# A two-layer hybrid decoder step: compression products spread over the first eight steps of prompt attention

## The chip, the cores and the metric

The kernel runs on one core of one Trainium2 chip, in float32. The metric is the device time of one launch in microseconds (us), taken as the median of several runs. A profiled execution is one more run, taken by the hardware profiler; its span is the time from its first to its last recorded instruction.

A core has five engines that matter here: TensorE (PE; its weight loads are PEld), VectorE (DVE), ScalarE (ACT), GpSimd (POOL) and SyncE (SP). Each works through its own queue of instructions in order; where an instruction needs another engine's result it waits on a semaphore, and everything behind it on that engine waits too. Data comes from device memory by DMA; here SyncE issues the loads of weights and GpSimd the gathers of the caches.

## The reference, cut to what matters

Two request groups share the weights: one prompt of 512 tokens, and 8 sampled sequences of 4 new tokens each, with 2048 past tokens in paged caches. Each of the two layers has a recurrent group (RG-LRU) beside an attention group with three branches, an output projection and a gated ConvFFN. What the change touches is the attention group, sampled and prompt:

```
def _compress(rows, pe, w1, b1, w2):            # 32 rows -> one compressed row, every 16 rows
    ua = einsum('bnshd,sdf->bnhf', ch + pe[:16], w1[:16])
    ub = einsum('bnshd,sdf->bnhf', ch + pe[16:], w1[16:])
    hid = gelu(ua[:, :-1] + ub[:, 1:] + b1)
    return einsum('bnhf,fd->bnhd', hid, w2)

def _nsa_core(...):
    p_cmp = masked_softmax(q_c . kc);  o_cmp = p_cmp . vc          # compressed rows
    idx = top_k(block sums of p_cmp, 16)
    o_slc = masked_softmax(q_r . ks[idx]) . vs[idx]                # selected blocks of 64 rows
    o_win = masked_softmax(q_r . kw) . vw                          # the last 512 rows
    return gates . (o_cmp, o_slc, o_win)
```

The sampled sequences compress their whole compressed-branch cache in every layer (8 sequences of 2048 rows), read all pages of the selected-branch cache, and mask the blocks that were not selected. The prompt compresses its own 512 rows.

## The kernel before, in words

**One layer.** Projections, RG-LRU and the key and value projections come first; then compression; then a planned stretch of attention; then the output projection and the ConvFFN. The dense products (line 377) take most of TensorE's time and are not touched.

**Compression.** The list `compressed_units` (line 283) has nine units: seven sampled caches ("cmp" 0 to 6), the prompt's own rows ("cmpp"), and the eighth sampled cache. For one sampled cache GpSimd issues four gathers into a 16 KB slot of `ar` (`cache`, line 1064; three slots in turn), VectorE transposes the rows in two instructions (`turn_chunks`, lines 1627 and 1633), and TensorE forms two products, v = 0 for keys and v = 1 for values, of 16 matmuls each (lines 497 and 498), into one of banks 6 and 7 of PSUM. ScalarE applies the gelu (line 1255), TensorE the second layer (`compress2`, line 511), and VectorE copies the result out (`second_layer`, line 1816). The prompt's unit reads its rows back from the output array, where SyncE has stored them; GpSimd waits for that store. In the order of TensorE each unit is product 0, the second layer of the unit before, product 1. The parts of the sampled compressed attention (`sample_cmp`, lines 617 and 1782: scores, group sums that choose the blocks, values) stand between units as `CMP_PARTS` says; the group sums and values of the second four sequences stand in steps 0 and 1 of the plan.

**The plan** (lines 309 to 345) is a list written out by loops; TensorE, VectorE, ScalarE and GpSimd each walk it in order and do their own part of every entry. Its steps n = -1 to 24 hold 22 prompt units: tile i of 128 queries has one unit of all 4 groups per branch for i = 0, two units of 2 for i = 1, and four of 1 for i = 2 and 3. A prompt unit begun in step n has its scores in step n (TensorE), then the maxima (`p_max`, VectorE, line 1864) and the exp (`p_exp`, ScalarE, line 1384); in step n + 1 the division by the sum and the gate (`p_weights` on VectorE, `weigh` on GpSimd, line 1118); in step n + 2 the transposes (TensorE, line 546) and copies (VectorE 1545, ScalarE 1396); in step n + 3 the values (TensorE, line 558). Compressed scores, transposes and values of a tile stand in the steps of its first unit (lines 577 to 586).

**Sampled units.** Six of them, three for each half G of four sequences: the window (`win`, one slot) and two pairs of selected-cache pages (`slc`, a slot per sequence). Each unit passes through keys (VectorE transposes them, 16 columns of 128 per slot, line 1918), scores in two halves (TensorE, then VectorE, line 1940, then ScalarE's exp, line 1415), turn (TensorE, line 692, and two copies), values, and, at the end of a half, output. `BASE` gives the step of each unit's first scores and `SAMPLE_PARTS` the offset of each part; keys stand one step ahead. After the values of a unit GpSimd issues the next gathers. Selected and window units use the three slots of `ar` and a fourth in `wr` (`a_slot`, line 295):

```
sample_units = [(G, e) for G in range(2) for e in (None, 0, 2)]
BASE = (0, 2, 6, 9, 11, 15)
SAMPLE_PARTS = {"keys": -1, "scores0": 0, "scores1": 1, "turn": 2, "values": 3, "output": 4}
CMP_PARTS = {4: ("scores", 0), 5: ("group", 0), 6: ("values", 0), 8: ("scores", 1)}
```

**Banks and weights.** PSUM has eight banks; `take` (line 358) hands them out by kind: scores in pairs from 0 to 3, products in 6 and 7 ("acc"), transposes, sampled values and the like in 4, 5 and 7 ("three"), the sum of a tile's values in 6 ("out"). Before the plan TensorE spreads the sampled queries (`qrep`) once. The copies of those (`qrep`), the scores of a sampled pair (`sQ`) and the causal mask lie in the columns of `w1`, the weights of the products; the scores of a window unit (`sW`) in those of the compressed keys. Weights have nine slots (line 262): 0 to 3 are the columns of `wr` that the fourth cache slot uses, 4 the columns behind them, 5 to 8 the third cache slot of `ar`. SyncE fetches weights in order (lines 998 to 1004), and for the eight output weights and the first of the ConvFFN it first waits until the cache slots there are used.

## Time and profile before

| what | value |
|---|---|
| median of 3 runs | 2300.4 us (2300.24 to 2300.83) |
| the profiled execution, its time | 2298.58 us |
| its span | 2296.8 us |
| mean granted clock of TensorE over the span | 0.952 of full speed |
| TensorE busy | 94% of the span |
| bytes moved by DMA | 205.22 MB, a mean of 89 GB/s |

How to read it: the profiled execution's time is 1.8 us under the median of the runs, and 1.8 us of it lie outside the span. Busy time counts an engine's instructions, not its waits. The granted clock is what the chip allowed TensorE, as a share of 2.4 GHz; the other level is half of it, so a mean between 0.5 and 1 is a share of time at each. In the rows below a line number such as L497 is a line of the kernel before, "x16" a count of instructions, and "out<-in" names the tiles written and read. A note in brackets at the end of a row is the idle time of that engine before the instruction, and what ended it.

### The profile page before, as it was taken

To read this page: it belongs to the slowest core of one execution; us is meant where nothing else is said; L and a number is where in the kernel's file an instruction comes from. 1 tells how busy PE (TensorE), PEld (TensorE's weight loads), DVE (VectorE), ACT (ScalarE), POOL (GpSimd) and SP (SyncE) were. 2 spreads that over 40 slices of the span, in tenths; PEclk is the share of its full clock that TensorE was granted. 3 is DMA by queue.
4 is the path that set the end of the run, shared out by engine and by line. 5 is a ranking of instruction groups with operands and counts; after the bars stand their busy time and mean duration, and the time that the engine had idled before them with its cause. 6 is when DMAs were issued, how large, how long until landed. Compare 5 with 4: busy or idle time off the path is not lost.

```text
span 2296.8 us, 30286 instructions
## 1 busy us (share of the span) xinstructions
PE 2165.2 (94%) x12250; PEld 1739.6 (76%) x12250; DVE 788.2 (34%) x1649; ACT 444.7 (19%) x1014; POOL 364.6 (16%) x486
## 2 busy tenths in 40 slices
PE   6999996878999999999999999788899999999997
PEld 5789884546888888888887988644578888888886
DVE  3455326563332022022345623456624211211214
ACT  2331013223211011011224111222332111100111
POOL 2000212425110000000200022133421000000002
PEclk8999996879999999999999999878899999999998
DMA  9204432342242222222131053322312222222211
GB/s 278 75 1 139 147 124 107 114 140 87 83 124 74 74 68 70 74 74 74 51 79 32 20 193 119 148 111 103 91 30 73 83 74 73 68 71 74 74 37 45
DMA packets 246634, 205.22 MB, mean 89 GB/s; under 512 B 26808, under 2 KB 232352, under 8 KB 244064
## 3 DMA queue, kind: packets, MB, share of 16 engines
q1 hardware_dynamic: 231680, 126.13, 19.4%
q0 software_dynamic: 14816, 77.15, 9.2%
q8 instruction: 98, 1.61, 0.3%
q14 instruction: 40, 0.33, 0.0%
HBM read 197.09 MB, written 14.48 MB: 92 GB/s over the span
## 4 chain that ended last, share of the span: by engine, by line
PE 85%; DVE 8%; issue 2%; ACT 2%; SPq 2%; POOL 0%; DMA 0%; DVEq 0%; ACTq 0%
PE ps L377 71%; PE ps L497 5%; PE ps L498 5%; PE ps L558 2%; DVE ar L1918 1%; PE ps L546 1%; DVE ov L1693 1%; DVE ps L1864 1%; ACT ov L1384 1%; SPq L925 1%; SPq L917 0%; DVE wr L1918 0%; DVE ov L1705 0%; PE ps L586 0%; DVE ts L1545 0%
## 5 line engine op out<-in xcount | busy, mean ns | idle before, releaser
L377 PE MATMUL ps<-hT,wr 128*128 128x272 f32 x2304 | 540.1, 395 | 7.6 <-DMA wr<-in_w_in 6.9
L377 PEld LDWEIGHTS ps<-hT,wr 128*128 128x128 f32 x2304 | 440.3, 191 | 100.2 <-DMA wr<-in_w_in 7.3
L377 PE MATMUL ps<-hT,ar 128*128 128x272 f32 x1792 | 417.2, 393 | 0.8 <-ACT ov L1316 0.6
L377 PEld LDWEIGHTS ps<-hT,ar 128*128 128x128 f32 x1792 | 340.1, 190 | 72.2 <-issue 2.4
L377 PE MATMUL ps<-ov,wr 128*128 128x272 f32 x1024 | 240.7, 392 | 0.0
L377 PEld LDWEIGHTS ps<-ov,wr 128*128 128x128 f32 x1024 | 193.9, 190 | 39.5
L2030 DVE TENSOR_SCALAR ov<-ov,par 128x560 f32<-128x560 f32 x48 | 27.4, 571 | 458.0 <-ACT ov L1479 437.7
L377 PE MATMUL ps<-ov,ar 128*128 128x272 f32 x768 | 180.1, 393 | 2.0 <-DVE hT L1906 2.0
L377 PEld LDWEIGHTS ps<-ov,ar 128*128 128x128 f32 x768 | 145.5, 190 | 32.1 <-issue 2.4
L497 PE MATMUL ps<-ar,w 128*128 128x256 f32 (+1 forms) x576 | 166.1, 370 | 0.0
L498 PE MATMUL ps<-ar,w 128*128 128x256 f32 (+1 forms) x576 | 164.7, 367 | 0.0
L1159 POOL COPY ov<-ov 128x2 f32<-128x2 f32 x48 | 9.1, 189 | 838.3 <-ACT ov L1479 838.3
L1476 ACT ACTIVATE ov<-ps 128x272 f32<-128x272 f32 x48 | 19.1, 398 | 566.8 <-PE ps L377 566.8
L1118 POOL TENSOR_SCALAR ov<-ov,sm 128x128 f32<-128x128 f32 (+3 forms) x92 | 94.9, 1045 | 175.0 <-DVE sm L1875 175.0
L498 PEld LDWEIGHTS ps<-ar,w 128*128 128x128 f32 x576 | 107.0, 190 | 13.2
L497 PEld LDWEIGHTS ps<-ar,w 128*128 128x128 f32 x576 | 105.3, 190 | 12.9 <-issue 0.8
L1081 POOL DMA_INDIRECT ar<-in_cache_cmp_kv,idi x64 | 60.9, 952 | 258.7 <-PE ps L377 124.9
L377 PE MATMUL ps<-ar,w 32*32 32x128 f32 (+1 forms) x896 | 93.7, 532 | 5.3 <-DVE ar L1918 5.3
L2039 DVE TENSOR_TENSOR ov<-ps,ov 128x544 f32<-128x544 f32 (+1 forms) x52 | 35.0, 680 | 179.8 <-PE ps L377 170.8
L1633 DVE STREAM_TRANSPOSE ar<-ar 128x2048 f32<-128x2048 f32 (+1 forms) x36 | 76.8, 2133 | 40.1 <-DMA ar<-in_cache_cmp_kv,idi 39.3
L1384 ACT ACTIVATE ov<-ps,sm 128x128 f32<-128x128 f32 (+3 forms) x92 | 45.9, 512 | 176.3 <-DVE sm L1864 174.5
L1561 DVE RECIPROCAL ps<-ps 128x272 f32<-128x272 f32 x16 | 29.9, 1866 | 144.6 <-ACT ps L1222 144.5
(314 smaller groups left out, 2243.5 us busy)
## 6 DMA issues: line engine op xcount, KB each, us to landing
wr<-in_ffn_w_in SPq DMA_DIRECT2D x53, 512.0 KB, 3.7
ar<-in_ffn_w_in SPq DMA_DIRECT2D x43, 512.0 KB, 3.7
wr<-in_ffn_w_down SPq DMA_DIRECT2D x27, 512.0 KB, 4.1
ar<-in_ffn_w_down SPq DMA_DIRECT2D x21, 512.0 KB, 4.1
ar<-in_cache_win_kv POOLq DMA_DIRECT2D x4, 2048.0 KB, 8.6
out_s_win<-in_cache_win_kv SPq DMA_DIRECT2D x16, 508.0 KB, 7.8
wr<-in_w_in SPq DMA_DIRECT2D x14, 512.0 KB, 3.6
ar<-in_w_in SPq DMA_DIRECT2D x12, 512.0 KB, 3.6
```

Source lines behind the costliest of these rows:

```text
L377: mm = lambda o, a, b, st, sp: nc.tensor.matmul(o, a, b, start=st, stop=sp)
L497: nc.tensor.matmul(oa, w1[:, v, sp, :], xa, start=first, stop=False, skip_group_check=True)
L498: i = nc.tensor.matmul(ob, w1[:, v, 8 + sp, :], xb, start=False, stop=sp == 7, skip_group_check=True)
L546: j = nc.tensor.transpose(pst[:, b, c * P:(c + 1) * P], p_slot(2 * n + h)[:, c * P:(c + 1) * P], ident)
L558: j = nc.tensor.matmul(pst[h * HD:(h + 1) * HD, b, g * P:(g + 1) * P], kvt[br][:, c, P + h * HD:P + (h + 1) * HD], tv(st[n, h])[:, k * P:( ...
L1081: po.indirect_dma_start(av(n)[:, c * 1024:(c + 1) * 1024], None, src, bass.IndirectOffsetOnAxis(ap=ixc, axis=0)).then_inc(sem(name), up(na ...
L1118: nc.gpsimd.tensor_scalar(pv, pv, sm[:, col:col + 1], None, ALU.mult).then_inc(sem("p_weighed"), up("p_weighed", (l, n, h)))
L1384: act(p_slot(m)[:, x * L:(x + 1) * L], pst[:, b + h, x * L:(x + 1) * L], ACT.Exp, scale=-1.0, bias=sm[:, mc:mc + 1], accum_out=sm[:, col:c ...
L1561: v(V.reciprocal(pst[:, b, 0:TH], pst[:, b, 0:TH]))
L1633: V.transpose(x[:, vv], x[:, vv]).then_inc(sem("chunks_turned"), up("chunks_turned", (u, vv)))
L2030: v(tsc(cF, gp[:, 0:560], cw(0), par[:, P_FCB + f:P_FCB + f + 1], ALU.mult, ALU.add))
L2039: tt(dst, src, gate, ALU.mult).then_inc(sem("act_ready"), up("act_ready", (l, f), frees=[("psum", (l, "u", f))]))
```

## The change

The nine compression units no longer run as a block ahead of the plan. The prompt's unit moves from the eighth place to the third. The plan begins with the six products of the first three units; the other twelve products stand in steps 0 to 7 behind the prompt scores of the step, one or two to a step in turn (`PIECES`). A second layer follows the first product of the next unit, the last one stands at the head of step 8, and there too the sampled queries are spread. All six sampled units move behind that: their first scores are in steps 8, 10, 13, 15, 17 and 20, their keys where `KEYS_AT` says. Within the first half the two pairs of selected slices now come before the window unit, in the second half the window stands between the pairs; the loads are gathered in that order. The first four sequences' compressed parts are in steps 4 to 6, the second four's in steps 8 to 10 (`CMP_AT`).

Products have one bank, 7, and the kind "three" has banks 4 and 5 until the spread and 4, 5 and 7 after it. The bank of a tile's values is opened by its first prompt unit, no longer by the compressed values, which now come behind it. Waits follow: TensorE waits for the window keys and roped queries at step 0, for the prompt's compressed keys and values where it uses them; ScalarE waits for the stored rows at its first exp, and for the prompt's second layer at the third. The causal mask moves to columns of `wr` in weight slot 4, so GpSimd writes it early, once the weight before is used. GpSimd issues the gathers of a unit at the first product of the unit two places ahead of it in the order, and those of the selected slices after the last second layer's place at the head of step 8. The output weights in `wr` wait for the second window unit, that in slot 4 for the last maxima, the rest for sequence 5's slice.

```diff
-        mask_row = lambda i: free1[:, 3104 + 384 - i * P:3104 + 512]
+        mask_row = lambda i: wr_flat[:, 4096 + 384 - i * P:4096 + 512]
...
-        compressed_units = lambda l: [(l, "cmp", x) for x in range(DB - 1)] + [(l, "cmpp", 0), (l, "cmp", DB - 1)]
+        compressed_units = lambda l: [(l, "cmp", 0), (l, "cmp", 1), (l, "cmpp", 0)] + [(l, "cmp", x) for x in range(2, DB)]
...
-                loads += [(l, "win", G)] + [(l, "slc", 4 * G + b) for b in range(4)]
+                loads += [(l, "slc", b) for b in range(4)] + [(l, "win", 0)] if G == 0 else [(l, "slc", 4), (l, "slc", 5), (l, "win", 1), (l, "slc", 6), (l, "slc", 7)]
...
-        sample_units = [(G, e) for G in range(2) for e in (None, 0, 2)]
-        BASE = (0, 2, 6, 9, 11, 15)
-        SAMPLE_PARTS = {"keys": -1, "scores0": 0, "scores1": 1, "turn": 2, "values": 3, "output": 4}
...
-        CMP_PARTS = {4: ("scores", 0), 5: ("group", 0), 6: ("values", 0), 8: ("scores", 1)}
+        sample_units = [(0, 0), (0, 2), (0, None), (1, 0), (1, None), (1, 2)]
+        closing_units = (2, 5)
+        BASE = (8, 10, 13, 15, 17, 20)
+        SAMPLE_PARTS = {"keys": 0, "scores0": 1, "scores1": 2, "turn": 3, "values": 4, "output": 5}
+        KEYS_AT = (7, 8, 13, 15, 16, 19)
+        PIECES = ((0,), (1, 2), (3,), (4, 5), (6,), (7, 8), (9,), (10, 11))
...
+        CMP_AT = {4: ("scores", 0), 5: ("group", 0), 6: ("values", 0), 8: ("scores", 1), 9: ("group", 1), 10: ("values", 1)}
         plan = []
-        for n in range(-1, NU + 3):
...
+        def compress_piece(x, v):
...
+            plan.append(("cmp", "product", (x, v)))
+            if x and v == 0:
+                plan.append(("cmp", "second", x - 1))
...
+        for x in range(3):
+            for v in range(2):
+                compress_piece(x, v)
+        for n in range(max(NU + 3, BASE[-1] + 5)):
             if 0 <= n < NU:
                 plan.append(("prompt", "scores", n))
+            for piece in PIECES[n] if n < len(PIECES) else ():
+                compress_piece(3 + piece // 2, piece % 2)
+            if n == len(PIECES):
+                plan.append(("cmp", "second", DB))
+                plan.append(("sample", "spread", (0, 0, None)))
             if 0 <= n - 1 < NU:
                 plan.append(("prompt", "weigh", n - 1))
...
-            if n == 0:
-                plan.append(("sample_cmp", "group", 1))
+            if n in CMP_AT and CMP_AT[n][0] != "values":
+                plan.append(("sample_cmp", *CMP_AT[n]))
...
-                    if n == BASE[k] + at and (part != "output" or e == 2):
+                    if n == (KEYS_AT[k] if part == "keys" else BASE[k] + at - 1) and (part != "output" or k in closing_units):
                         plan.append(("sample", part, (k, G, e)))
+            if 0 <= n - 3 < NU:
+                plan.append(("prompt", "values", n - 3))
             for i in range(4):
                 if n == first_unit[i] + 3:
                     plan.append(("tile", "values", i))
-            if 0 <= n - 3 < NU:
-                plan.append(("prompt", "values", n - 3))
...
-                                   "three": ((4, 5, 7), "three", 1), "out": ((6,), "out", 1)}[kind]
+                                   "three": ((4, 5, 7) if late_banks[0] else (4, 5), "three", 1), "product": ((7,), "product", 1), "out": ((6,), "out", 1)}[kind]
...
-                    hb = take((u, "hid", v), "acc")
+                    hb = take((u, "hid", v), "product")
...
-                    b = take((u, "c2", v), "quad")
+                    b = take((u, "c2", v), "three")
...
+                    if n == 0:
+                        pe.wait_ge(sem("kT_copied"), after("kT_copied", (l, "w")))
+                        pe.wait_ge(sem("q_roped"), after("q_roped", (l, 3)))
...
-                    b = S.bank_of[l, i, "O"]
+                    b = take((l, i, "O"), "out") if n == first_unit[i] else S.bank_of[l, i, "O"]
...
+                    pe.wait_ge(sem("comp_keys_ready"), after("comp_keys_ready", l))
...
+                    pe.wait_ge(sem("vbd_built"), after("vbd_built", l))
...
+                    elif what == "spread":
+                        late_banks[0] = True
+                        spread_queries()
...
-                if 0 <= n - unit_no[l, "out", 0] < NW and n % NW != 4:
-                    for s, n_ in freed(("a", load_no[l, "slc", 5 if n % NW < 4 else 4])):
+                if 0 <= n - unit_no[l, "out", 0] < NW and n % NW == 4:
+                    sp.wait_ge(sem("neg_max"), after("neg_max", (l, NU - 1)))
+                elif 0 <= n - unit_no[l, "out", 0] < NW:
+                    for s, n_ in freed(("a", load_no[(l, "win", 1) if n % NW < 4 else (l, "slc", 5)])):
                         sp.wait_ge(s, n_)
...
-                cache(l * A0 + NCMP + NA)
-                po.wait_ge(sem("compressed"), after("compressed", (compressed_units(l)[-1], 1)))
+                for w in range(unit_no[l, "out", 0] - NW, unit_no[l, "out", 0]):
+                    if w % NW == 4:
+                        for s, n_ in freed(("w", w)):
+                            po.wait_ge(s, n_)
                 nc.gpsimd.memset(mask_row(3)[:, 0:384], 0.0).then_inc(sem("mask_ready"), up("mask_ready"))
...
-                    if (who_, what) == ("prompt", "weigh"):
+                    if what == "product" and n[1] == 0:
+                        cache(l * A0 + n[0] + 2)
+                    elif (what, n) == ("second", DB):
+                        cache(l * A0 + NCMP + NA)
+                    elif (who_, what) == ("prompt", "weigh"):
                         weigh(n)
                     elif (who_, what) == ("sample", "values"):
-                        cache(l * A0 + NCMP + (4, 6, 8, 9, 9, 9)[n[0]])
+                        cache(l * A0 + NCMP + (5, 7, 8, 9, 9, 9)[n[0]])
...
+                    if n == 0:
+                        ac.wait_ge(sem("kv_stored_c"), after("kv_stored_c", l))
+                    if n == 2:
+                        ac.wait_ge(sem("compressed2"), after("compressed2", (us[2], 1)))
...
+                    if what == "product":
+                        x, v = n
+                        hidden_layer(us[x], v, us[x - 1] if x else (l - 1, "cmp", DB - 1) if l else None)
...
-                        if k >= 2 and not half:
-                            before = (l, "win", 0) if e is None else (l, "pair", *sample_units[k - 1]) if sample_units[k - 1][1] is not None else (l, "pair", *sample_units[k - 2])
-                            ve.wait_ge(sem("turned"), after("turned", (before, "ptn")))
+                        if G and not half:
+                            ve.wait_ge(sem("turned"), after("turned", ((l, "win", 0) if e is None else (l, "pair", 0, e), "ptn")))
...
+                    if what == "product":
+                        if n[1] == 0 and 0 < n[0] < DB:
+                            turn_chunks(us[n[0] + 1])
+                    elif what == "second":
+                        second_layer(us[n])
```

## Rows read from the trace of the kernel before

**Rows 1.** The page: its first line, TensorE's busy time, the chain by engine.
```profile
span 2296.8 us, 30286 instructions
...
PE 2165.2 (94%) x12250; PEld 1739.6 (76%) x12250; DVE 788.2 (34%) x1649; ACT 444.7 (19%) x1014; POOL 364.6 (16%) x486
...
PE 85%; DVE 8%; issue 2%; ACT 2%; SPq 2%; POOL 0%; DMA 0%; DVEq 0%; ACTq 0%
```

**Rows 2.** Table of stretches: length, busy time (count) by engine, TensorE's clock, DMA share, GB/s.
```profile
214.30:346.10 131.80, 130.60 (x710) 111.56 (x709) 40.18 (x60) 15.14 (x29) 28.91 (x34) 1.00 0.43 145
346.10:437.10 91.00, 69.82 (x697) 44.09 (x697) 56.32 (x181) 25.02 (x87) 29.66 (x37) 0.68 0.28 109
437.10:528.30 91.20, 74.72 (x791) 44.96 (x789) 55.34 (x149) 27.72 (x62) 29.51 (x23) 0.81 0.38 122
528.30:556.50 28.20, 22.52 (x250) 16.00 (x246) 14.49 (x45) 10.86 (x24) 18.35 (x14) 1.00 0.03 8
214.30:556.50 342.20, 297.67 (x2440) 216.60 (x2439) 166.33 (x434) 78.74 (x202) 106.44 (x108) 0.87 0.34 118
1333.50:1675.80 342.30, 297.86 (x2440) 214.78 (x2439) 166.07 (x434) 78.81 (x202) 103.74 (x104) 0.87 0.35 118
```

**Rows 3.** Timeline, compression of layer 0: start, length, engine and line, tiles, count.
```profile
310.95 0.65 PE L497 MATMUL ps<-ar,w 128*128 128x256 f32 x2
...
312.71 4.66 DVE L1633 STREAM_TRANSPOSE ar<-ar 128x2048 f32<-128x2048 f32 x2 [1.21 <-DMA ar<-in_cache_cmp_kv,idi]
...
317.91 0.27 PE L633 MATMUL ps<-cst,hT 128*127 128x128 f32 x1
...
318.16 0.47 ACT L1255 ACTIVATE hid<-ps,sm 128x254 f32<-128x254 f32 x1 [7.03 <-PE ps L498]
...
318.29 0.29 DVE L1545 COPY ts<-ps 127x128 f32<-127x128 f32 x1 [0.92 <-PE ps L633]
...
319.04 0.32 PE L497 MATMUL ps<-ar,w 128*128 128x62 f32 x1
...
322.75 0.44 PE L377 MATMUL ps<-hid,w 128*64 128x127 f32 x4
...
323.61 0.39 PE L497 MATMUL ps<-ar,w 128*128 128x62 f32 x2
```

**Rows 4.** Timeline, ScalarE at the end of compression: table load and exp.
```profile
344.28 1.28 ACT L1368 ACT_TABLE_LOAD   x1 [1.62 <-DVE sm L1787]
...
345.58 0.37 ACT L1368 ACTIVATE hT<-ps,sm 128x127 f32<-128x127 f32 x1
```

**Rows 5.** Timeline, TensorE in steps 3 to 6, at clock 1.00.
```profile
395.40 1.09 PE L586 MATMUL ps<-ts,ov 128*64 128x128 f32 x16
...
396.32 1.04 PE L558 MATMUL ps<-ts,ov 128*64 128x128 f32 x16
...
397.30 1.13 PE L377 MATMUL ps<-ov 64*128 64x256 f32 x8
...
398.36 1.09 PE L546 MATMUL ps<-cst,hT 128*128 128x128 f32 x8
...
415.87 0.98 PE L377 MATMUL ps<-hT,ov 64*128 64x32 f32 x16
```

**Rows 6.** Around step 10: a stretch of 20 us, keys, the wait for copies.
```profile
460.00:480.00 20.00, 13.13 (x75) 5.29 (x79) 11.29 (x24) 3.26 (x10) 2.76 (x3) 0.58 0.19 82
...
462.71 2.31 DVE L1918 STREAM_TRANSPOSE wr<-wr 128x2048 f32<-128x2048 f32 x1
...
467.49 0.40 PE L683 MATMUL ps<-cst,kcT 128*32 128x128 f32 x1 [5.46 <-DVE ts L1545]
```

**Rows 7.** DMA issues: KB each, median us to landing.
```profile
out_p_cmp<-ov SPq DMA_DIRECT2D x1, 512.0 KB, 5.1
...
ar<-in_cache_slc_kv,idi POOLq DMA_INDIRECT x4, 10.5
```

**Rows 8.** Table of stretches: 20 us in which SyncE loads the output weights.
```profile
500.00:520.00 20.00, 17.37 (x129) 7.71 (x124) 14.08 (x32) 3.98 (x10) 6.21 (x4) 0.83 0.90 237
```

More of the change, by code:

```diff
@@ L354, in _ @@
         def _(pe):
-            cyc = {"pair": 0, "one": 0, "acc": 0, "quad": 0, "half": 0, "stat": 0, "three": 0, "out": 0}
+            cyc = {"pair": 0, "one": 0, "acc": 0, "quad": 0, "half": 0, "stat": 0, "product": 0, "three": 0, "out": 0}
+            late_banks = [False]
             def take(key, kind):
```

151 lines of the change are left out of this document (69 added, 82 removed).

## The prediction, made before the change was run

> **What bounds the kernel now.** I read the page first, then a table of stretches, then single instructions. The page shows TensorE busy for 94% of the span and 85% of the chain that ended last on it [rows 1], so time is to be won only where TensorE is idle or runs at the lower clock. The table of stretches [rows 2] finds that place. Compression of layer 0 takes 131.8 us with TensorE busy for 130.6 of them at granted clock 1.00: nothing is lost there. The next 91.0 us are steps 0 to 7 of the plan: busy 69.82 at clock 0.68. Then 91.2 us hold steps 8 to 17: busy 74.72 at 0.81; and 28.2 us hold steps 18 to 24, which have almost no sampled work: busy 22.52 at 1.00. The whole is 342.2 us, and 342.3 in layer 1, so one layer is worked out and taken twice. Busy time by granted clock gives the work at full clock (2.4 GHz): 130.6 + 47.5 + 60.5 + 22.5 = 261.1 us. So 81 us of each layer's 342.2 are idle time or half clock, none of it in compression. The change can win at most that.
>
> **The new order in three stretches.** F holds the six first products, B steps 0 to 7 with the other twelve products, C steps 8 to 24 with all six sampled units.
>
> *F.* A product of a sampled page takes 317.91 - 310.95 = 6.96 us, one of the prompt's 322.75 - 319.04 = 3.71, a second layer 323.61 - 322.75 = 0.86 [rows 3]. Products had two banks and now have one (7), so each waits for the gelu of the one before: some 0.25 us after the product, 0.47 long [rows 3], and 0.25 until TensorE goes on (taken equal to the way there), 1.0 together. Where ScalarE must first change its table, 1.28 are added [rows 4], 2.25 together. F is 4 x 6.96 + 2 x 3.71 + 2 x 0.86 + waits (2.25 + 1.0 + 0.1 + 1.0, two being covered by a second layer) = 41.3. The prompt's unit is now third and reads back rows that SyncE stores as F begins: the store lands 5.1 us after its issue [rows 7], inside the first product, and the unit is needed after four. GpSimd, which waits for it, then waits for the second product's end anyway before it may gather again. So this costs nothing; if the store were late, all later gathers would be too.
>
> *B, work.* Twelve products 83.5, six second layers 5.2. Prompt instructions at full clock [rows 5]: eight scores of up to 1.13 (9.0), six transposes of 1.09 (6.5), five values of 1.04 (5.2), three compressed scores of 0.98 (2.9), two compressed values of 1.09 (2.2); the small rest 2 (an estimate from the pieces of 0.27 and 0.86 us in rows 3). Together 116.5.
>
> *B, waits.* Steps 1, 3, 5 and 7 run two products. ScalarE did an exp just before, so the second waits the 2.25 us with a table load; in steps 3 and 7 a second layer hides 0.86 of it: 7.3. Below, this wait is nothing if the gelu were ready; above, 2.25 four times. In step 0 the copy for the prompt's second layer stands on VectorE behind a page's transposes: 1.5, an estimate, bounded by nothing and by those two transposes (4.66, rows 3). Until the spread there are two banks instead of three for transposes, second layers and their like: a transpose after a second layer waits for its copies, six times 0.6 (a copy of 0.29, rows 3, and its way). B is 116.5 + 12.4 = 128.9, F and B 170.2. What took 131.8 + 91.0 = 222.8 us thus takes 52.6 less, because products run where TensorE waited for softmax.
>
> On the table load the row shows 1.28 us with the exp 0.02 us behind it [rows 4]. By the Trainium skill, ScalarE: Activation LUTs, section "What ACT_TABLE_LOAD costs", a switch costs about 2.66 us, as a drain of 1.38 goes with the load. By that rule, which the row does not bear out, each of the four waits is an estimated 1.38 us longer and the sum 11 us higher for both layers.
>
> *C.* Its work is 261.1 - (41.3 - 4.35 + 116.5) = 107.6 us, against 83.0 in the same steps before: the sampled chain is whole here. The price of its gaps comes from one that the trace has. From 460 to 480 VectorE transposed the next pair's keys (2.31 us a slot) ahead of copies that TensorE needed; TensorE stood 5.46 us and the clock fell, so that 20 us hold 13.13 x 0.58 = 7.6 us of work [rows 6]. The rest of steps 8 to 17 is (60.5 - 7.6) / (91.2 - 20) = 0.743 work per us. So C without such a hole is 107.6 / 0.743 = 144.8 us, and a hole adds 20 - 7.6 / 0.743 = 9.8.
>
> How many? Keys of a unit of pages are 4.62 us of VectorE. In step 7 products cover them. In step 8 the gathers of slots 2 and 3 can start only after the last product and land 10.5 us later [rows 7]; then come the transposes, then the maxima of step 9, and behind them the group sums that TensorE waits for at the head of step 9: one hole. In step 15 keys and first scores of one unit stand in the same step, so TensorE waits for the whole transposition: one hole. In step 13 it is the same with a window unit, one slot of 2.31 us: short. In step 19 the last gather is issued a step earlier only, but its scores come in step 20: short. I take two: C = 164.4.
>
> *Sum.* 170.2 + 164.4 = 334.6 against 342.2, 7.6 less a layer, 15.3 in both. The profiled execution lasted 2298.58 us, which gives 2283.3. It lies 1.8 under the median of the three runs, so I forecast 2285.
>
> *At no cost.* The eight output weights and the channel mixer's first are fetched later: slots in wr once the second window unit is used (step 20, not 14), slot 4 once step 21's maxima are done, and SyncE waits in order. Earlier 20 us at 237 GB/s moved such an amount [rows 8]; four steps of some 9 us (91.2 for ten, rows 2) cover it, and if not, the output projection starts late by up to that difference. Mask and zero fill of GpSimd move ahead and are short; behind the four gathers that GpSimd issues for a unit stand the weighings, which TensorE needs two steps later. TensorE's waits for keys and roped queries at step 0, ScalarE's for the stored rows and for the prompt's second layer, and the wait for compressed keys end with work that is earlier in their queues; the last is part of the 1.5 above. The output bank is now opened by the prompt's values instead of the compressed ones: the same instructions in another order.
>
> **Rivals.** With h holes a layer takes 170.2 + 144.8 + 9.8 h.
> - *Dense C*, h = 0: the gathers land in time and prompt work fills the rest. 315.0, 27.2 less a layer, so 2246. For it: steps 18 to 24 reach 0.80 work per us [rows 2]. Against it: they have hardly any key transposes.
> - *The key transposes decide*, h = 4: steps 8, 13, 15 and 19 each stop TensorE as in rows 6, with the clock at its lower level (1.2 GHz) behind. 354.2, 12.0 more a layer: 2324, slower. It decides from h = 2.8. For it: steps 0 to 7 of before, with two such units and little other work, hold 47.5 / 91.0 = 0.52 per us. Against it: steps 13 and 19 wait for less.
> - *Break-even*, h = 2.8: what F and B win, C gives back; 2300.
> - *The table switch costs double*: each of the four waits a layer pays 1.28 twice, which adds 10.2 us, 2295. Against it is the exp at 345.58 right behind its load [rows 4]. It is the case in which the page of the Trainium skill named above were right about the drain.
>
> **Chances.** The forecast (h from 1.5 to 2.5) 0.42, dense C (h under 1.5) 0.18, break-even 0.08, table switch 0.04, key transposes (h over 3) 0.28. A difference of 0.2%, 4.6 us, is about what a measurement of this kernel can tell from no change. So faster 0.60, same 0.12, slower 0.28. The forecast's own range is 2275 to 2295. With no waits in F and B and h = 0 it would be 2212, with the waits doubled and h = 4 it would be 2358; the range leaves out these ends and reaches from below dense C to the slower rival: 2240 to 2322.
>
> **What would show it.** Right: from the first product to step 8's scores about 170 us at clock near 1.00, with gaps of 2 us before the second product of steps 1, 3, 5 and 7; two idle spells of over 5 us on TensorE, at the group sums of step 9 and before the scores of the fourth sampled unit, each followed by half clock; 164 us from there to the output projection. Wrong: a clock under 0.95 in B (then products wait for chunks or banks that I cost at nothing), other idle spells over 5 us in C, above all in the steps after 21, where no prompt scores are left, or an output projection that waits for weights.

## The result, and the profile after

The changed kernel takes 2354.8 us (median of 4 runs, 2354.7 to 2359.4) against 2300.6 us for the kernel before beside it: a ratio of 1.0237, 95% interval 1.022 to 1.0255. It is 54 us slower; the forecast was 2285.

The page of the profile after: its first two lines, and two groups of TensorE (busy time, mean ns, then the idle time ahead of them and who ended most of it).

```profile
span 2353.0 us, 30314 instructions
...
PE 2199.1 (93%) x12250; PEld 1757.5 (75%) x12250; DVE 788.9 (34%) x1649; ACT 480.5 (20%) x1042; POOL 365.1 (16%) x486
...
L517 PE MATMUL ps<-ar,w 128*128 128x256 f32 (+1 forms) x576 | 176.4, 390 | 19.5 <-ACT hid L1285 19.2
...
L397 PE MATMUL ps<-ar,w 32*32 32x512 f32 (+1 forms) x704 | 92.8, 679 | 23.0 <-DVE ar L1947 22.7
```

Against [rows 1], TensorE runs as many instructions and is busy 33.9 us longer, so the same work ran at a lower clock; the rest of the 56 us of span is idle time. ScalarE has 28 instructions more and 35.8 us more work, which is 28 table loads of 1.28 us. The two groups name the two places where TensorE now stands: the products wait 19.2 us for gelus (0.0 before), and the sampled units' scores 22.7 us for VectorE's key transposes (5.3 before in the group of 32*32 products of the same tiles).

The table of stretches after, with the prediction's cuts (columns as in [rows 2]): F, B and C of layer 0, then F and B together and C of layer 1.

```profile
215.10:258.20 43.10, 39.77 (x209) 33.89 (x208) 8.10 (x13) 4.22 (x8) 9.72 (x12) 0.96 0.41 135
258.20:396.50 138.30, 124.00 (x738) 101.30 (x737) 61.90 (x167) 48.03 (x113) 45.23 (x54) 0.95 0.26 92
396.50:582.00 185.50, 149.71 (x1498) 87.58 (x1496) 96.79 (x255) 44.49 (x95) 51.02 (x40) 0.75 0.33 117
...
1359.00:1546.50 187.50, 170.10 (x944) 141.16 (x943) 69.94 (x180) 52.26 (x121) 54.80 (x66) 0.92 0.29 99
1546.50:1732.00 185.50, 145.42 (x1498) 85.36 (x1496) 96.41 (x255) 44.48 (x95) 48.55 (x37) 0.76 0.33 117
```

| stretch | forecast | layer 0 | layer 1 |
|---|---|---|---|
| F and B: first product to the scores of step 8 | 170.2 | 181.4 | 187.5 |
| C: scores of step 8 to the output projection | 164.4 | 185.5 | 185.5 |
| a layer (342.2 before) | 334.6 | 366.9 | 373.0 |

So both parts came out too long, 28.5 us over both layers in F and B and 42.2 in C. The timeline after shows the stops of C. In the fence: step 9 of layer 0, its step 15, its step 17, and step 20 of layer 1 (start, length, engine and line, tiles, count, and in brackets the idle time before and what ended it).

```profile
406.11 7.05 PE L397 MATMUL ps<-ar,w 32*32 32x512 f32 x32
...
414.67 2.31 DVE L1947 STREAM_TRANSPOSE ar<-ar 128x2048 f32<-128x2048 f32 x1
...
417.02 2.31 DVE L1947 STREAM_TRANSPOSE wr<-wr 128x2048 f32<-128x2048 f32 x1
419.37 0.69 DVE L1935 COPY hT<-ps 128x512 f32<-128x512 f32 x1
420.09 0.57 DVE L1893 CUSTOM_DVE_ANT_0 ps<-ps,wr 128x384 f32<-128x384 f32 x1
...
422.05 0.33 DVE L1832 TENSOR_SCALAR hT<-hT,sm 128x127 f32<-128x127 f32 x1
...
422.52 0.77 PE L397 MATMUL ps<-hT,cst 128*128 128x127 f32 x2 [5.88 <-DVE hT L1832]
...
494.71 4.66 DVE L1947 STREAM_TRANSPOSE ar<-ar 128x2048 f32<-128x2048 f32 x2
...
499.52 4.49 PE L397 MATMUL ps<-ar,w 32*32 32x512 f32 x20 [5.54 <-DVE ar L1947]
...
519.66 2.31 DVE L1947 STREAM_TRANSPOSE wr<-wr 128x2048 f32<-128x2048 f32 x1
...
525.40 0.73 PE L720 MATMUL ps<-cst,w 64*128 64x64 f32 x8 [4.49 <-DVE ts L1584]
...
1682.10 3.11 POOL L1146 TENSOR_SCALAR hT<-hT,sm 128x512 f32<-128x512 f32 x2 [9.04 <-DVE sm L1904]
...
1685.57 1.00 POOL L1112 DMA_INDIRECT ar<-in_cache_slc_kv,idi  x1 [0.36 <-issue]
...
1697.27 2.31 DVE L1947 STREAM_TRANSPOSE ar<-ar 128x2048 f32<-128x2048 f32 x1 [3.03 <-DMA ar<-in_cache_slc_kv,idi]
...
1699.73 3.31 PE L397 MATMUL ps<-ar,w 32*32 32x512 f32 x14 [4.07 <-DVE ar L1947]
```

In each of the four, key transposes end what TensorE waits for, or stand on VectorE ahead of it. In step 9 two of them, a copy and the step's maxima come before the small operation that the group sums need; what each is worth there, experiment 2 shows. In step 15 the scores wait for 4.66 us of them outright. In step 17 one stands ahead of the copy that gives a bank back. In step 20 of layer 1 the last slice was gathered late, behind a weighing on GpSimd. The first row shows what the clock does between the stops: 32 matmuls of a sampled unit take 7.05 us here, and 3.64 in a run below where the clock stayed at its upper level.

### The profile page after: what moved, and what is told of

It reads as the page before. It is cut to its first block and busy times, and to the rows that moved or that the text cites. A ratio compares the mean times of both kernels' runs of the same rounds, so it can differ in the third digit from the quotient of the medians.

```text
span 2353.0 us, 30314 instructions
## 1 busy us (share of the span) xinstructions
PE 2199.1 (93%) x12250; PEld 1757.5 (75%) x12250; DVE 788.9 (34%) x1649; ACT 480.5 (20%) x1042; POOL 365.1 (16%) x486
## 5 line engine op out<-in xcount | busy, mean ns | idle before, releaser
L517 PE MATMUL ps<-ar,w 128*128 128x256 f32 (+1 forms) x576 | 176.4, 390 | 19.5 <-ACT hid L1285 19.2
L518 PE MATMUL ps<-ar,w 128*128 128x256 f32 (+1 forms) x576 | 172.4, 383 | 0.0
L517 PEld LDWEIGHTS ps<-ar,w 128*128 128x128 f32 x576 | 110.3, 201 | 43.7 <-ACT hid L1285 24.2
L518 PEld LDWEIGHTS ps<-ar,w 128*128 128x128 f32 x576 | 112.9, 201 | 14.8
L397 PE MATMUL ps<-ar,w 32*32 32x512 f32 (+1 forms) x704 | 92.8, 679 | 23.0 <-DVE ar L1947 22.7
L2075 DVE TENSOR_TENSOR ov<-ps,ov 128x544 f32<-128x544 f32 (+1 forms) x52 | 35.0, 680 | 179.8 <-PE ps L397 170.8
L1672 DVE STREAM_TRANSPOSE ar<-ar 128x2048 f32<-128x2048 f32 (+1 forms) x36 | 76.8, 2134 | 22.7 <-DMA ar<-out_p_cmp 19.5
L1893 DVE CUSTOM_DVE_ANT_0 ps<-ps,wr 128x128 f32<-128x128 f32 (+3 forms) x128 | 59.9, 518 | 70.3 <-PE ps L397 43.8
```

The lines of the kernel that those rows point to most:

```text
L397: mm = lambda o, a, b, st, sp: nc.tensor.matmul(o, a, b, start=st, stop=sp)
L517: nc.tensor.matmul(oa, w1[:, v, sp, :], xa, start=first, stop=False, skip_group_check=True)
L518: i = nc.tensor.matmul(ob, w1[:, v, 8 + sp, :], xb, start=False, stop=sp == 7, skip_group_check=True)
L1672: V.transpose(x[:, vv], x[:, vv]).then_inc(sem("chunks_turned"), up("chunks_turned", (u, vv)))
L1893: V.tensor_tensor_reduce(out=sv, in0=sv, in1=mask_row(i), scale=-1.0, scalar=3.0e38, op0=ALU.add, op1=ALU.min, accum_out=sm[:, mc:mc + 1]) ...
L2075: tt(dst, src, gate, ALU.mult).then_inc(sem("act_ready"), up("act_ready", (l, f), frees=[("psum", (l, "u", f))]))
```

## The experiments

Each was timed beside the kernel before (2300.0 to 2301.9 us). Ratios are to that kernel, with 95% intervals; differences to the changed kernel (2354.8 us) are between medians. The tables of stretches have the columns of [rows 2], and their cuts are those of the table above.

**1. Undo the spreading alone** (2385.7 us, ratio 1.0385, 1.0354 to 1.0417).

```diff
-        for x in range(3):
+        for x in range(DB + 1):
             for v in range(2):
                 compress_piece(x, v)
+        plan.append(("cmp", "second", DB))
...
-            for piece in PIECES[n] if n < len(PIECES) else ():
-                compress_piece(3 + piece // 2, piece % 2)
```

> All 18 products stand ahead of step 0 again, in the new order and with the one bank; everything else, the sampled chain from step 8 too, is that of the changed kernel (2354.8 us). Theory 1 (the products do fill TensorE's waits for softmax in steps 0 to 7, and what is lost is lost behind step 8): steps 0 to 7 then hold prompt work alone, some 33 us of it in 8 steps of 7 to 9 us, so the first product to step 8 takes 135 + 56 to 72 = 191 to 207 us a layer instead of 181, and behind step 8 nothing moves: 2375 to 2407 us. Rival (the spread products cost as much as they hide, by table loads, the one bank and half clock): 2345 to 2365 us.

Layer 0, first product to the scores of step 8, and from there to the output projection:

```profile
213.80:412.00 198.20, 170.84 (x954) 140.95 (x954) 69.12 (x180) 32.63 (x106) 53.88 (x65) 0.91 0.33 115
412.00:602.90 190.90, 151.78 (x1489) 88.15 (x1487) 97.95 (x255) 43.52 (x95) 51.72 (x41) 0.72 0.26 92
```

The first stretch is 198.2 us instead of 181.4, as theory 1 has it. Without the spreading the new order is 84 us slower than the kernel before, and the spreading gives 31 of them back: that half of the forecast's mechanism holds. Behind step 8 the two layers together take 4.4 us more than in the changed kernel (190.9 and 184.5 us). What costs more than the spreading gains is the rest of the new order, above all behind step 8: these 190.9 us stand against 119.4 for steps 8 to 24 of before, though part of the difference is the work of the chain that moved there.

**2. Leave the key transposes out** (2300.7 us, ratio 0.9997, 0.9982 to 1.0012).

```diff
-                            V.transpose(x, x).then_inc(sem("keys_turned"), up("keys_turned", n))
+                            V.transpose(x[:, 0], x[:, 0]).then_inc(sem("keys_turned"), up("keys_turned", n))
```

> Of the sampled keys only the first of 16 column sets is transposed in each slot (the scores of the sampled units are then of wrong keys), so VectorE has 10 x 2.2 = 22 us less a layer behind step 7; gathers, waits and TensorE's work stay. Theory 1 (VectorE's key transposes stand in front of what TensorE needs, and half clock follows each stop): the stops of 5.9, 3.0, 5.5 and 1.7 to 4.1 us shrink to 1 to 2 and some 10 us of half clock a layer go with them, 18 to 24 us a layer: 2307 to 2319 us. Rival (late gathers or the length of the sampled chain itself set these stops): under 6 us a layer, 2343 to 2355 us.

C of both layers, and the group sums of step 9 in layer 0:

```profile
393.50:555.80 162.30, 137.57 (x1497) 81.04 (x1496) 76.93 (x254) 44.49 (x95) 50.97 (x40) 0.81 0.38 134
1519.50:1684.20 164.70, 139.11 (x1498) 81.76 (x1496) 76.44 (x254) 44.48 (x95) 48.47 (x37) 0.80 0.38 132
...
409.98 0.46 PE L397 MATMUL ps<-hT,cst 128*128 128x127 f32 x2 [4.61 <-DVE hT L1832]
```

It gains 54 us, more than theory 1's 36 to 48; the profiled execution took 2307.0 us, and C gives 44.0 of its 47.8 less. C is 23.2 and 20.8 us shorter, for 20 us of VectorE work. In layer 0, TensorE's idle time falls by 11.1 us (35.8 to 24.7) and its busy time, at the same count, by 12.1: stop and lower clock weigh alike. Not all stops went: the group sums still stand 4.61 of their 5.88 us, since the copy and the maxima of the step remain ahead of them.

**3. Fill the waits with matmuls** (2349.6 us, ratio 1.023, 1.0195 to 1.0265), then with half as many (2314.4 us, ratio 1.0061, 1.004 to 1.0081).

```diff
+            def warm(b, count):
+                for _ in range(count):
+                    nc.tensor.matmul(pst[:, b, :], ident, cst[:, 0:512], start=True, stop=True)
...
                     b = take((l, G, "gsum"), "three")
+                    warm(b, 12 * G)
```

The second run has 6 in place of 12 at this wait; the other waits likewise.

> TensorE runs matmuls whose results are overwritten (128 x 128 weights, 512 columns, some 0.44 us each at full clock, 3 to 12 of them, 45 a layer) into the bank that it has just taken, ahead of eight of its waits behind step 8: what was idle there is filled, nothing else changes. Theory 1b (the lower clock behind step 8 comes from the idle spells): of the 41.6 us a layer that half clock costs there, 15 to 25 come back, less 2 to 4 us where a filler runs on past its wait: 2312 to 2333 us. Rival (the 32 x 32 matmuls of the sampled units run at the lower clock whatever stands ahead of them): no gain, 2352 to 2363 us.

> The filled run had twice the filler it was meant to have: each filler took 0.88 us, not 0.44, so behind step 8 it cut half clock from 41.6 to 3.9 us in layer 0 and idle time from 35.8 to 17.0, but brought 51.7 us of filler work. Here 27 fillers a layer instead of 57, 23.8 us in waits of 24 to 28. Theory 1b (the lower clock follows the idle spells and costs what rows say): half clock behind step 8 under 12 us a layer again, filler work some 24 in place of 19 of idle, so 20 to 27 us a layer less than the changed kernel: 2300 to 2315 us. Rival (VectorE's queue sets the pace behind step 8, so that what TensorE saves in clock becomes longer waits): 2330 to 2350 us.

The first run's filler around the scores of the first sampled unit (7.05 us at 406.11 in the changed kernel), the filler at the group sums, then C of layer 0; below it C of both layers of the second run.

```profile
398.64 4.54 PE L401 MATMUL ps<-cst 128*128 128x512 f32 x6 [1.91 <-DVE kcT L1878]
...
404.92 3.64 PE L397 MATMUL ps<-ar,w 32*32 32x512 f32 x32
...
410.36 10.57 PE L401 MATMUL ps<-cst 128*128 128x512 f32 x24
...
393.00:573.90 180.90, 163.87 (x1612) 90.18 (x1610) 96.85 (x255) 44.46 (x95) 50.96 (x40) 0.97 0.34 121
```

```profile
398.00:568.90 170.90, 153.86 (x1552) 85.20 (x1550) 96.38 (x255) 44.49 (x95) 51.08 (x40) 0.88 0.36 128
1527.60:1688.30 160.70, 141.45 (x1552) 80.38 (x1550) 96.40 (x255) 44.49 (x95) 48.54 (x37) 0.96 0.41 135
```

The first fillers were mis-sized: each float32 matmul of 512 columns is two records and 0.88 us, so 12 fill 10.57 us where 5.88 were idle, and there were 57 a layer, not 45. With 27 a layer the time falls by 40 us, though TensorE has 24 us a layer more to do. The lower clock is thus not in the nature of the sampled units' matmuls: their 32 take 3.64 us when TensorE has been busy ahead of them. In these two runs it follows the stops. Of the first run both theories missed the time; of the second it lies at the top of theory 1b's range.

**4. Keys a step earlier** (2334.4 us, ratio 1.0138, 1.0121 to 1.0155).

```diff
-        KEYS_AT = (7, 8, 13, 15, 16, 19)
+        KEYS_AT = (7, 8, 12, 14, 16, 19)
```

> The keys of the first window unit stand in step 12 instead of 13 and those of the fourth unit in step 14 instead of 15, a step ahead of their scores. Prediction's own price: a hole less (9.8 us a layer) and the short one at 13 too (3 us): 12 us a layer, 2325 to 2335 us. Rival (VectorE's queue is full there, the same transposes then stand ahead of other copies and maxima, or wait for their gathers): within 8 us of the changed kernel, 2347 to 2363 us.

Layer 0, step 14:

```profile
487.66 4.66 DVE L1947 STREAM_TRANSPOSE ar<-ar 128x2048 f32<-128x2048 f32 x2
...
496.51 0.40 PE L711 MATMUL ps<-cst,kcT 128*32 128x128 f32 x1 [5.05 <-DVE ts L1584]
```

It gains 20 us of the 24 that the forecast's prices give, not the rival's nothing. But the number agrees and the mechanism does not: in the timeline of layer 0 the stop of 5.54 us in step 15 is gone, and one of 5.05 stands just ahead of it (1.97 there before), ahead of the window unit's last transpose, where a bank waits for a copy that is now behind those 4.66 us of transposes. The block moved; it did not get smaller. In the profiled execution, the slowest of its four (2344.1 us), C is 6.4 and 10.0 us shorter, of which 2.1 and 4.9 are idle time and the rest a higher clock.

**5. The block cut in two** (2308.6 us, ratio 1.0043, 1.0026 to 1.006).

```diff
-        KEYS_AT = (7, 8, 13, 15, 16, 19)
+        KEYS_AT = ((6, 7), (8, 9), (12,), (13, 14), (16,), (18, 19))
...
+                for x, at in enumerate(KEYS_AT[k]):
+                    if n == at:
+                        plan.append(("sample", "keys%d" % x, (k, G, e)))
...
-                        for n in [load_no[u]] if e is None else [load_no[l, "slc", 4 * G + e + x] for x in range(2)]:
+                        for n in [load_no[u]] if e is None else [load_no[l, "slc", 4 * G + e + int(part[4])]]:
```

> The changed kernel with the key transposes of a pair's two slots in two steps, 2.3 us each, instead of 4.6 us in one, and none in the step of its scores: steps 6 and 7, 8 and 9, 12 (window), 13 and 14, 16 (window), 18 and 19. Work and counts stay. Theory 1 (what stops TensorE is how much transposing stands at one place of VectorE's queue): the stops of 5.9, 3.0, 5.5 and 1.7 to 4.1 us a layer become 3 or less each, with their half clock 12 to 20 us a layer less than the changed kernel and more than the run with keys a step earlier alone (2334.4) gave: 2315 to 2330 us. Rival (VectorE's sum of work behind step 8 sets the pace, wherever the transposes stand): 2334 us or more.

C of both layers, and the wait that stood 5.05 us in experiment 4:

```profile
397.10:558.30 161.20, 131.61 (x1497) 80.54 (x1495) 94.55 (x254) 44.48 (x95) 50.96 (x40) 0.84 0.38 135
1516.50:1684.20 167.70, 139.83 (x1497) 84.14 (x1495) 94.11 (x254) 44.48 (x95) 48.57 (x37) 0.79 0.37 130
...
478.89 0.40 PE L714 MATMUL ps<-cst,kcT 128*32 128x128 f32 x1 [2.87 <-DVE ts L1587]
```

It gains 46 us, more than expected, with VectorE as busy as ever but for one transpose moved ahead of C (94.55 us against 96.79). C is about as short as in experiment 2, where the work was left out. So it is not the sum of VectorE's work that costs, but where it stands and how much of it at one place of the queue. The two are not wholly parted: the edit also moves transposes by a step, and experiment 4, which only moves two units, gave 20 of the 46 us. What the cut does by itself one wait shows: with 2.31 us of transposing ahead of it instead of 4.66 it stands 2.87 us instead of 5.05. Nor did all stops fall to 3 us, as theory 1 had it: in layer 0 the group sums still stand 5.16 us and the turn in step 17 still 4.50. There 6.2 of the 24.3 us that C lost were idle time and 18.1 a higher clock.

**6. The same cut in the kernel before** (2267.1 us, ratio 0.9853, 0.9837 to 0.9869).

```diff
+        KEYS_AT = ((-1,), (0, 1), (4, 5), (8,), (9, 10), (13, 14))
```

The rest of the edit is as in experiment 5.

> The kernel before with the same split: keys of its pairs in steps 0 and 1, 4 and 5, 9 and 10, 13 and 14, one slot each. Theory 1: the stop of 5.5 us at step 10 and part of the 17 us of half clock behind it go, and the stop of 2.6 us at step 15: 5 to 10 us a layer, 2281 to 2291 us. Rival (steps 0 to 10 are paced by VectorE and softmax together): 2296 to 2305 us.

The whole layer 0, and the wait that answers to the last row of [rows 6]:

```profile
214.70:542.20 327.50, 290.47 (x2440) 213.42 (x2439) 166.39 (x434) 78.71 (x202) 106.41 (x108) 0.89 0.36 123
...
457.95 0.39 PE L687 MATMUL ps<-cst,kcT 128*32 128x128 f32 x1 [3.12 <-DVE ts L1549]
```

This version beats both kernels: 33 us under the kernel before, 88 under the changed one. A layer takes 327.5 us instead of 342.2, 7.5 less idle (44.5 to 37.0) and 7.2 less busy at the same count. The miss: 14.7 us a layer, not 5 to 10. The stop of 5.46 us did not go but lost 2.34, about the length of one slot's transposition (2.31), and that of 2.63 in step 15 went as expected; but a stop of 5.11 us in step 2 also lost 2.34, and one of 3.17 in step 6 went. Another, at the second half's compressed values, grew from 4.25 to 5.59.

**7. Filler in the kernel before** (2299.9 us, ratio 0.9992, 0.9983 to 1.0002).

```diff
                     b = take((u, "S", half), "two")
+                    warm(b, 0 if half else {0: 7, 5: 3}.get(k, 0))
...
                     b = take((l, G, "Ocs"), "quad")
+                    warm(b, (0, 4)[G])
```

> The kernel before with 14 fillers a layer (12.3 us) ahead of the scores of its first window unit (7), of the values of the second half's compressed rows (4) and of the scores of its last pair (3), where TensorE stood 6.3, 4.3 and 2.6 us. Theory 1b: the 41 us of half clock that follow the first of these stops (20.5 us of time) shrink to under 25 (12.5), 6 to 12 us a layer less than before: 2277 to 2289 us. Rival (steps 0 to 7 are set by VectorE and softmax, the clock only stretches what waits anyway): 2297 to 2305 us.

Layer 0, the wait of 6.32 us and the filler behind it:

```profile
357.75 0.80 PE L377 MATMUL ps<-hT,cst 128*128 128x127 f32 x2 [6.33 <-ACT ov L1390]
358.34 7.45 PE L381 MATMUL ps<-cst 128*128 128x512 f32 x14
```

No gain: the time is the rival's. But the run does not decide between the two. The longest stop is that of the second half's group sums, not of the window unit's scores behind them, so the seven fillers (14 records) stand behind it and it still lasts 6.33 us; half of the filler is work on top. The two other stops were filled (0.98 us are left of 4.25, nothing of 2.63). In the table of stretches the clock of layer 0 is 0.90 instead of 0.87 and of layer 1 0.89, and the layers take 339.0 and 342.6 us. What sets the pace in steps 0 to 7 of the kernel before these fillers leave open; experiment 6 names the key transposes as a part of it.

**8. Splitting and filling together** (2311.3 us, ratio 1.0045, 1.0022 to 1.0068).

```diff
                     b = take((l, G, "gsum"), "three")
+                    warm(b, (0, 5)[G])
...
                     b = take((l, G, "Ocs"), "three")
+                    warm(b, (0, 2)[G])
```

This stands on the kernel of experiment 5; at the turns of the second, fourth and last unit there are 1, 4 and 2 more.

> The changed kernel with split keys (2308.6 us) and 14 fillers a layer (12.3 us) in the stops that are left behind step 8: group sums of the second half (5 fillers in 5.2 us), its values (2 in 1.8), turns of the second, fourth and last unit (1, 4 and 2 in 1.6, 4.5 and 2.0). If half clock is a cost of its own beside VectorE's transposes: the 24 to 33 us a layer of it behind step 8 halve, 10 to 16 us a layer less: 2277 to 2289 us. If the two were one and the same loss, paid once: 2300 us or more.

C of layer 0 is 167.6 us, of layer 1 167.1:

```profile
397.90:565.50 167.60, 145.30 (x1525) 82.06 (x1524) 94.54 (x254) 44.49 (x95) 50.93 (x40) 0.85 0.37 130
```

Two of the waits that fillers were meant for, in layer 0:

```profile
430.72 2.65 PE L404 MATMUL ps<-cst 128*128 128x512 f32 x4 [2.83 <-DVE ts L1595]
...
510.18 5.40 PE L404 MATMUL ps<-cst 128*128 128x512 f32 x8 [4.41 <-DVE ts L1595]
```

Nothing on top of the split, where the expectation reads one and the same loss. The trace does not carry that reading. At the compressed values and at the turn of the fourth unit TensorE waits for the copy that gives the bank back into which the fillers write, so those six of the 14 stand behind the wait (2.83 and 4.41 us are left) and come on top. And the clock of C is 0.85 in both layers against 0.84 and 0.79 with the split alone: in layer 0 half clock was not taken away. Whether the gains of experiments 3 and 5 are one loss or two stays open.

**9. Exp in place of the gelu** (2317.4 us, ratio 1.0091, 1.0059 to 1.0123).

```diff
-                          ACT.Gelu_apprx_tanh, bias=sm[:, 140 + v:141 + v]).then_inc(sem("hidden"), up("hidden", (u, v), frees=[("psum", (u, "hid", v))]))
+                          ACT.Exp, bias=sm[:, 140 + v:141 + v]).then_inc(sem("hidden"), up("hidden", (u, v), frees=[("psum", (u, "hid", v))]))
```

> The changed kernel with exp in place of the gelu in the hidden layer (other values; the same shapes), so that ScalarE changes its table far less between products and softmax. Prediction's price of the four second products of a layer with a table load, 1.28 us each: 5.1 us a layer, with the half clock behind them up to 8: 2339 to 2345 us. The rival with the doubled load: 10 us a layer and more, 2335 us or less. If gelus are hidden anyway: 2352 us or more.

F and B of both layers, then the wait of step 5 in the changed kernel (timelines of ScalarE and TensorE):

```profile
215.10:381.70 166.60, 157.45 (x946) 130.76 (x945) 70.16 (x180) 30.34 (x104) 55.00 (x66) 0.99 0.32 110
1341.50:1508.10 166.60, 157.36 (x944) 130.77 (x943) 70.08 (x180) 30.35 (x104) 54.86 (x66) 0.99 0.32 112
```

```profile
342.98 1.28 ACT L1285 ACT_TABLE_LOAD   x1 [3.38 <-issue]
344.28 0.47 ACT L1285 ACTIVATE hid<-ps,sm 128x254 f32<-128x254 f32 x1
...
344.80 1.07 PE L517 MATMUL ps<-ar,w 128*128 128x256 f32 x2 [1.89 <-ACT hid L1285]
```

ScalarE has 17 instructions fewer in the stretch and 21.9 us less work: 17 table loads. F and B take 166.6 us instead of 181.4 and 187.5, so these loads cost 14.8 and 20.9 us a layer. Of the 14.8, 8.5 were idle time (17.6 to 9.2) and 6.3 the busy time of the same 946 matmuls at a lower clock; of the 20.9 in layer 1, 8.2 and 12.7. The single wait is near the forecast's 2.25: 1.89 us, with a load of 1.28 and the gelu 0.02 behind it. The prediction's price was too low by far; the time lies in the band of the rival with the doubled load, but no row shows a doubled load: what doubles the price is the clock behind the waits; and 17 loads went, of which the forecast priced five.

**10. Products in four steps** (2326.6 us, ratio 1.0116, 1.0095 to 1.0136), with filler (2309.6, 1.003, 1.0008 to 1.0053), and with split keys (2303.8, 1.0012, 0.9996 to 1.0029).

```diff
-        BASE = (8, 10, 13, 15, 17, 20)
+        BASE = (5, 7, 11, 13, 16, 19)
-        KEYS_AT = (7, 8, 13, 15, 16, 19)
+        KEYS_AT = (4, 6, 10, 12, 15, 18)
-        PIECES = ((0,), (1, 2), (3,), (4, 5), (6,), (7, 8), (9,), (10, 11))
+        PIECES = ((0, 1, 2), (3, 4, 5), (6, 7, 8), (9, 10, 11))
-        CMP_AT = {4: ("scores", 0), 5: ("group", 0), 6: ("values", 0), 8: ("scores", 1), 9: ("group", 1), 10: ("values", 1)}
+        CMP_AT = {1: ('scores', 0), 2: ('group', 0), 3: ('values', 0), 4: ('scores', 1), 5: ('group', 1), 6: ('values', 1)}
...
```

> The twelve spread products stand three to a step in steps 0 to 3, the compressed sampled parts in steps 1 to 6 (their values behind the prompt's values of the step), and the sampled units' first scores in steps 5, 7, 11, 13, 16 and 19, keys in 4, 6, 10, 12, 15 and 18, so that the chain has the prompt units of steps 5 to 22 beside it. Theory 1 (behind step 8 the chain had too few prompt units beside it, and keys in the step of their scores): idle time and half clock behind the products fall from 77 us a layer towards the 37 that the kernel before had from step 8 on, and steps 0 to 3 pay two more table loads than gaps hidden: 10 to 25 us a layer less, 2305 to 2335 us. Rival (three products in a step stall on the one bank and its gelu, and the prompt's softmax then waits behind gelus): 2355 us or more.

> The kernel with products in four steps (2326.6 us) and 19 fillers a layer (16.7 us) ahead of the group sums (2 and 8), the second half's compressed scores (1) and values (5) and the turn of the fourth unit (3), where it stood 2.6, 7.9, 2.0, 5.5 and 3.5 us. Theory 1b: half clock behind the products falls from 32.5 us a layer by 10 to 20, 2290 to 2308 us. Rival (VectorE sets the pace): 2320 to 2332 us.

> The kernel with products in four steps (2326.6 us) with the same split: keys in steps 3 and 4, 5 and 6, 10, 11 and 12, 15, 17 and 18. Theory 1: its stops of 7.9, 5.5, 5.2 and 3.5 us lose 2.3 us each where a second transpose stood there, and half clock with them: 8 to 14 us a layer, 2298 to 2311 us. Rival: 2320 us or more.

Layer 0 of the first of them, first product to the scores behind the last one, and from there to the output projection:

```profile
213.70:376.90 163.20, 147.27 (x792) 122.40 (x791) 55.36 (x131) 32.78 (x84) 42.01 (x52) 0.96 0.34 117
376.90:568.70 191.80, 156.29 (x1652) 95.36 (x1649) 111.19 (x303) 53.63 (x124) 64.50 (x54) 0.80 0.32 112
```

With three more prompt units beside the chain and 10.3 us less of ScalarE's work (86.4 in place of 96.7: eight table loads), layer 0 takes 355.0 us instead of 366.9; which of the two gave how much, the run does not part. The second stretch still holds 35.5 us of idle time. Filler gave 17 us and the split 23. None of this design's versions came under the kernel before.

## Why the prediction was wrong, step by step

**F, near the forecast.** 43.1 us in layer 0 against 41.3: its waits measured 1.89, 0.6 and 0.6 where 2.25, 1.0 and 1.0 stood, but the clock was 0.96. In layer 1 the waits are the same, and F takes 47.6 at clock 0.86. The prompt's unit in third place cost no wait, as said.

**B: the work and the waits for gelus right, the lower clock left out.** It took 138.3 us in layer 0, 9.4 more than forecast. The four second products waited 1.35 to 1.89 us, 6.5 in all, against 7.3. The 1.5 us in step 0 and the six waits of 0.6 for banks were not there; in their place five stops of 1.3 to 1.9 us stood at the compressed parts and the transposes beside them, 7.7 in all against 5.1. What failed is that B was priced at clock near 1.00: it was 0.95, which is 6.2 of the 9.4 us (5% of 124.0 busy), and 0.94 in layer 1, under the prediction's own sign of being wrong. Nor do products in the place of softmax waits account for all that F and B save against the 222.8 us of before: of the 41.4 in layer 0, experiment 1 gives the spreading 16.8; the rest was saved with all products ahead of step 0, where the sampled units had left steps 0 to 7. The forecast's 6.4 us a layer for table loads (four of 1.28 and the first one) was 14.8 and 20.9 by experiment 9, idle time and clock together: the waits were sized about right, the clock behind them was the term at nothing. The rival with the doubled load had the right culprit and the wrong mechanism: the load itself takes 1.28 us, and the Trainium skill's drain of 1.38 us beside it (ScalarE: Activation LUTs, "What ACT_TABLE_LOAD costs") is in no row here, before or after.

**C: the base density failed, not the price of the holes.** I took C without holes as 144.8 us, from 0.743 of work per us in steps 8 to 17 of before without the 20 us around step 10. With only a sixteenth of the key transposing left, C still takes 162.3 and 164.7 us (experiment 2). These 18 to 20 us are the term that was mis-sized. By busy time and clock, layer 0's 162.3 are 111 us of work, 26 lost to the lower clock and 25 idle; the 144.8 held 107.6 of work and 37 for both losses. So the density of a stretch with part of the chain did not hold for the whole chain: it has stops that transposes are not the main part of, such as the 4.61 us of the group sums. How much of this comes from the fewer prompt units beside the chain, no run isolates.

The key transposes add 23.2 and 20.8 us, where two holes were priced at 19.6. That this fits is in part luck. Of the two stops that I named, the scores of step 15 (5.54 us) came as said; the group sums of step 9 (5.88) came mostly for another reason, as only 1.27 of them goes with the transposes. A third at step 17 (4.49), behind the second window unit's keys, and in layer 1 a fourth at step 20 (4.07), I had not. That the last gather would be short held in layer 0 only (1.67). The keys of step 7 are not covered by products either: TensorE waits 1.90 us at the head of step 8 for a copy behind them (1.69 in layer 1).

**The rival that ended slower was nearest, by luck in part.** By its own formula C gives h = (185.5 - 144.8) / 9.8 = 4.2, and it said 2324. It named the culprit that experiments 2, 4 and 5 show, the key transposes. But at 9.8 a hole they are worth 2.1 to 2.4 holes, not four; the other 18 us that make h come out at 4.2 are the base. The 31 us by which the run is slower still are F and B (28.5). I gave it 0.28 and the forecast 0.42, on the argument that steps 13 and 19 wait for less. They did (2.98 and, in layer 0, 1.67 us); steps 16 and 17 were not looked at. And the range ended at 2322, just short of this rival's own 2324, with the longer waits that I had priced for F and B left out.

**What was taken at nothing and was nothing.** The output weights: the projection's wait of 1.64 us ends with VectorE's copy, not with a load. The mask, the moved waits of ScalarE and the output bank show in no stop.

## What to carry to other kernels

When work is moved behind other work, don't price its new place with the busy share of a stretch that had another mix beside it: count what stays beside it, wait by wait. On an engine that serves two chains in order, cut a long operation into the pieces that the chains can stand, and put each where nobody waits; here cutting and placing together were worth nearly as much as leaving the operation out, and 1.5% on the kernel that was already faster. And where two functions of ScalarE alternate, each wait has the clock behind it as a second price, so a sum that prices only the wait was about half of it here (8.5 of 14.8 us, 8.2 of 20.9). Before you judge an experiment that fills waits, look in its trace whether the filler stands in the wait or behind it: an operation cannot fill the wait for the bank that it writes itself.

## What the runs showed of the hardware

A filler matmul in an idle spell is not free of charge but can pay: 24 us of extra work a layer made the changed kernel 40 us faster over two layers, as matmuls behind it ran at the upper level (in the first filled run 3.64 us in place of 7.05 for the same 32). On top of the split and in the kernel before it gained nothing, but there about half of it stood behind the waits. A float32 matmul of 512 columns counts as two records of 0.44 us.

And the same instructions in F and B took 181.4 us in layer 0 and 187.5 in layer 1 of one execution, at clock 0.95 and 0.92. The difference is one more fall of the clock, during the prompt's products, the last of F. It follows the same wait of 0.61 us in both layers; in layer 0 its matmuls go on at the upper level, in layer 1 pairs of them take 0.63 us instead of 0.39, from 1396.3 to about 1410:

```profile
249.65 0.43 PE L517 MATMUL ps<-ar,w 128*128 128x62 f32 x2 [0.61 <-ACT hid L1285]
...
254.80 0.39 PE L518 MATMUL ps<-ar,w 128*128 128x62 f32 x2
...
1393.54 0.43 PE L517 MATMUL ps<-ar,w 128*128 128x62 f32 x2 [0.61 <-ACT hid L1285]
...
1399.61 0.63 PE L517 MATMUL ps<-ar,w 128*128 128x62 f32 x2
```

Some 13 us at half clock cost 6 to 7. In the seven traces that have these products in these places, F and B took 179.8 to 183.4 us in nine of 14 layers and 185.8 to 187.6 in five. Why the clock fell in one layer and not in the other is open; a term of a few us that rests on the clock should be read from several layers and executions.
